# Decoder trunk step on one core: query columns first, cache pages on a fixed chunk schedule, value pages in pairs, softmax matmuls beside them, entry in pieces

## The reference, cut to what matters

```python
def branch_inputs(h, w_in, b_f, pos):
    z = h @ w_in
    rq, rk, rv, rg, fq, fk, fv, ff, gr, gf = jnp.split(z, cuts, axis=-1)
    ...
    logf = jax.nn.log_sigmoid(ff.astype(jnp.float32) + b_f.astype(jnp.float32))

def fox_sample(q, k_new, v_new, logf_new, k_past, v_past, logf_past):
    c = jnp.cumsum(jnp.concatenate([logf_past, logf_new], axis=1), axis=1)
    ...
    sc = jnp.concatenate([s_past, s_new], axis=-1) * (D_F ** -0.5) + c_q[..., None] - c_t[:, :, None, :]
    p = jax.nn.softmax(sc, axis=-1)
    return p[..., :p_len] @ v_past + p[..., p_len:] @ v_new

def trunk_layer(h, p, pos, attend, w_in, b_f, gn_g, w_ret_proj, w_fox_proj, w_out, ...):
    o_r, s_new, o_f = attend(rq, rk, rv, fq, fk, fv, logf)
    y_r = (group_norm(o_r) * silu(rg)) @ w_ret_proj
    y_f = o_f @ w_fox_proj
    mix = (sigmoid(gr) * y_r + sigmoid(gf) * y_f) @ w_out
    x1 = layer_norm(ALPHA * h + mix)
    ffn = (silu(x1 @ w1) * (x1 @ w3)) @ w2
    y = layer_norm(ALPHA * x1 + ffn + sigmoid(x1 @ w_pg) * (p @ w_pe))
```

## Time and profile before

| | us |
|---|---|
| median of 3 runs | 1923.43 |
| lowest and highest | 1921.81, 1926.93 |
| profiled execution, device time | 1920.19 |
| its span, first to last instruction | 1918.6 |
| PE busy | 1799.1 (94%) |
| DVE busy | 1024.2 (53%) |
| ACT busy | 777.3 (41%) |
| mean granted clock of PE | 0.978 |
| data moved by DMA | 386.18 MB |

### The profile page before, as it was taken

The page is one execution under the profiler, slowest core; times in us unless marked ns, Lnnn a source line. Parts: engine busy times, 40 slices in busy tenths (PEclk is TensorE's granted clock), DMA queues, the critical chain, the costliest instruction groups (busy, mean ns, idle before and its releaser), DMA issues.

```text
span 1918.6 us, 39299 instructions
## 1 busy us (share of the span) xinstructions
PE 1799.1 (94%) x14307; PEld 1730.0 (90%) x14307; DVE 1024.2 (53%) x2115; ACT 777.3 (41%) x906; POOL 149.1 (8%) x262
## 2 busy tenths in 40 slices
PE   5999989899788989999979999999999999999996
PEld 4999989789777877899969999999999999999995
DVE  5444575665656556456555544444444444444454
ACT  2443433334334333334335455555433334343333
POOL 3340101111122112000000000000000000000000
PEclk9999999899899999999989999999999999999998
DMA  5555667787799999545525555555555655555551
GB/s 159 148 159 162 210 225 249 232 305 239 238 366 334 310 350 338 187 149 186 180 65 176 169 186 176 183 180 180 176 179 177 188 180 175 179 182 166 180 180 46
DMA packets 318256, 386.18 MB, mean 201 GB/s; under 512 B 16376, under 2 KB 293368, under 8 KB 317784
## 3 DMA queue, kind: packets, MB, share of 16 engines
q1 hardware_dynamic: 286832, 287.48, 47.3%
q0 software_dynamic: 28352, 95.84, 14.1%
q10 hardware_dynamic: 2992, 1.79, 0.4%
HBM read 371.21 MB, written 13.84 MB: 201 GB/s over the span
## 4 chain that ended last, share of the span: by engine, by line
PE 79%; DVE 6%; issue 5%; DMA 5%; ACT 3%; POOLq 1%; ACTq 0%; DVEq 0%; POOL 0%; SPq 0%
PE acc L510 24%; PE acc L511 24%; PE acc L515 24%; DMA stateS<-in_state_ret 2%; ACT whi L451 2%; DMA page<-in_cache_v 1%; DVE pagesum L1235 1%; PE X L633 1%; PE X L808 1%; PE X L490 1%; DMA out_ret_state_sample<-stateS 1%; ACT stateS L1004 1%; DVE wlo L456 1%; PE X L483 1%; DVE stateS L1351 0%
## 5 line engine op out<-in xcount | busy, mean ns | idle before, releaser
L456 DVE TENSOR_TENSOR wlo<-raw,whi 128x1024 fp32r<-128x1024 f32 (+1 forms) x552 | 659.5, 1203 | 711.8 <-ACT whi L451 705.6
L451 ACT ACTIVATE whi<-raw 128x1024 fp32r<-128x1024 f32 (+1 forms) x552 | 569.3, 1038 | 701.8 <-PE acc L515 698.8
L510 PE MATMUL acc<-x_hi,whi 128*128 128x264 f32 x1664 | 415.5, 285 | 10.5 <-DVE x_lo L1483 6.8
L511 PE MATMUL acc<-x_lo,whi 128*128 128x264 f32 x1664 | 414.8, 285 | 0.0
L510 PE MATMUL acc<-hT_hi,whi 128*128 128x264 f32 x1408 | 374.9, 300 | 0.0
L511 PE MATMUL acc<-hT_lo,whi 128*128 128x264 f32 x1408 | 362.8, 292 | 0.0
L510 PEld LDWEIGHTS acc<-x_hi,whi 128*128 128x128 f32 x1664 | 313.7, 188 | 11.6 <-issue 7.2
L511 PEld LDWEIGHTS acc<-x_lo,whi 128*128 128x128 f32 x1664 | 315.0, 189 | 0.0
L510 PEld LDWEIGHTS acc<-hT_hi,whi 128*128 128x128 f32 x1408 | 276.1, 196 | 23.3 <-issue 20.2
L511 PEld LDWEIGHTS acc<-hT_lo,whi 128*128 128x128 f32 x1408 | 276.9, 197 | 0.6 <-issue 0.5
L515 PE MATMUL acc<-x_hi,wlo 128*128 128x264 f32 x1664 | 238.9, 286 | 0.0
(11 more groups left out here) (306 smaller groups left out, 1592.7 us busy)
## 6 DMA issues: line engine op xcount, KB each, us to landing
raw<-in_w SPq DMA_DIRECT2D x256, 512.0 KB, 4.0
raw<-in_w_in SPq DMA_DIRECT2D x176, 512.0 KB, 4.9
page<-in_cache_k POOLq DMA_DIRECT2D x64, 512.0 KB, 5.7
page<-in_cache_v POOLq DMA_DIRECT2D x64, 512.0 KB, 6.1
raw<-in_w_out SPq DMA_DIRECT2D x32, 512.0 KB, 4.5
raw<-in_w_pg SPq DMA_DIRECT2D x32, 512.0 KB, 3.5
stateS<-in_state_ret POOLq DMA_DIRECT2D x8, 1024.0 KB, 8.8
out_ret_state_sample<-stateS POOLq DMA_DIRECT2D x8, 1024.0 KB, 6.6
```

Of the source, the lines that this page charges most:

```text
L451: nc.scalar.activation(whi[:, s, 0:k, :], raw[:, s, 0:k, :], ACT.Copy).then_inc(S["hi_made"], 1)
L456: nc.vector.tensor_tensor(wlo[:, s, 0:k, :], raw[:, s, 0:k, :], whi[:, s, 0:k, :].bitcast(F32), ALU.subtract).then_inc(S["lo_made"], 1)
L510: mm(acc[c.acc][:, m, 0:T], w, xh[:, c.kt0 + t, :], start=c.first and t == 0, stop=False)
L511: mm(acc[c.acc][:, m, 0:T], w, xl[:, c.kt0 + t, :], start=False, stop=False)
```

## The change

- A phase `phQ` of 16 chunks does all query columns first; `phKV` (16 to 47) does keys and values. Later phases keep their chunk numbers.
- The laps are replaced by a table of due chunks. For token m the key pages are at chunks 24 + 16m + 1, 3, 5, 7, 9, 11, 12, 13, the bias and maximum at +14, its transpose at +15, the diagonal made at +16 and spread at +19, the exponential at +21, the sums at +22 and +23, the probabilities at +24, and pairs of value pages at +27, +31, +35, +39. The last pair is at chunk 175.
- Key pages have two buffers and value pages two of their own.
- States are handled every 7 chunks from chunk 112, with load at +0, scaling at +3, update and store at +5, use at +6; the sample tail follows at chunks 168 to 175 and `own_values` after the second chunk of `phYR`. The loops of `phG` are unrolled.
- x is loaded in half tiles, sample rows first. ACT computes the sample rows' mean and variance. PE does chunks 0 to 3 between the transposes, then the forget logits as 48 matmuls with the 8 columns of `wff` as weights.
- The 64 `Lc` loads are issued by SP, eight after each weight load from 4 to 11, instead of by POOL.

```diff
+FIRST, LAP = 24, 16
+KEY_AT = (1, 3, 5, 7, 9, 11, 12, 13)
+BIAS_AT, TURN_AT, TOP_AT, ROWS_AT, LESS_AT, EXP_AT, SUM_AT, SUMS_AT, PROB_AT = 14, 15, 16, 19, 20, 21, 22, 23, 24
+VALUE_AT = (27, 31, 35, 39)
+STATE0, STATE_LAP = 112, 7
+SCALE_AT, NEW_AT, OUT_AT = 3, 5, 6
...
-        phF = Phase(plan, 2, heads([FK, FQ, FV], 512, ready=lambda k: ("h_lo", k)))
+        phQ = Phase(plan, 1, heads([FQ], 1024, ready=lambda k: ("h_lo", k)))
+        phKV = Phase(plan, 2, heads([FK, FV], 512))
...
+            for j in range(len(phQ.chunks)):
+                load(phQ, 0, j)
+                if j == 4:
+                    sp.wait_ge(S["ptab_in"], 16)
+                if 4 <= j < 12:
+                    for i in range((j - 4) * 8, (j - 3) * 8):
+                        number = sp.value_load(ptab[0:1, i:i + 1], min_val=0, max_val=NPOOL - 1)
+                        sp.dma_start(Lc[:, i, :], a["cache_logf"][ds(number, 1)].rearrange("o s h -> s (o h)")).then_inc(S["past_in"], 16)
...
+            def forget_logits():
+                pe.wait_ge(S["h_made"], DT)
+                pe.wait_ge(S["wff_made"], 1)
                 for k in range(DT):
-                    last = mm(X[0:n, 0, t * 8:t * 8 + 8], h32[:, k, lo:lo + n], wff[:, k, :], start=k == 0, stop=k == DT - 1)
-            last.then_inc(S["ff_ps"], 1)
...
+                    mm(X[0:H_F, 0, 0:T], wff_hi[:, k, :], hT_hi[:, k, :], start=k == 0, stop=False)
+                    mm(X[0:H_F, 0, 0:T], wff_hi[:, k, :], hT_lo[:, k, :], start=False, stop=False)
+                    last = mm(X[0:H_F, 0, 0:T], wff_lo[:, k, :], hT_hi[:, k, :], start=False, stop=k == DT - 1)
+                last.then_inc(S["ff_ps"], 1)
...
+            def sample_step(c):
+                for n, at in enumerate(VALUE_AT):
+                    m = due(c, at)
+                    if m is not None:
+                        past_values(m, 2 * n)
+                        past_values(m, 2 * n + 1)
+                m = due(c, TURN_AT)
+                if m is not None:
+                    past_max_T(m)
...
+            h_tiles(0, 8)
+            for j in range(len(phQ.chunks)):
+                multiply(phQ, 0, j)
+                if j == 0:
+                    h_tiles(8, 12)
+                if j == 1:
+                    h_tiles(12, 16)
+                if j == 3:
+                    forget_logits()
+                    side_rows()
+                if j == 4:
+                    forget_rows()
...
-            act.wait_ge(x_in[1], 16)
+            act.wait_ge(x_in[0], 16)
...
+            xs, rest = xtok[0:DEC, 2, :], h32[0:DEC, 0:8, :].rearrange("p k t -> p (k t)")[:, 0:D]
+            link.step(A(rest, xs, ACT.Copy, accum_out=stat[0:DEC, 50:51]))
+            link.step(A(stat[0:DEC, 51:52], stat[0:DEC, 50:51], ACT.Copy, scale=-1.0 / D))
+            link.step(A(rest, xs, ACT.Square, bias=stat[0:DEC, 51:52], accum_out=stat[0:DEC, 52:53]))
...
+            h_rows(0, 4)
+            split_lo(dve, phQ, 0, 0)
+            h_rows(4, 8)
+            normalise(2)
+            split_lo(dve, phQ, 0, 1)
+            normalise(3)
...
+            def load_key(n):
+                if n >= 2:
+                    pool.wait_ge(S["page_used"], HEADS + (n - 1) * H_F)
+                number = pool.value_load(ptab[0:1, n:n + 1], min_val=0, max_val=NPOOL - 1)
+                pool.dma_start(page[:, n % 2, :], a["cache_k"][ds(number, 1)].rearrange("o s c -> s (o c)")).then_inc(page_in[n % 2], 16)
+
+            def load_value(n):
+                if n >= 2:
+                    pool.wait_ge(S["pv_ps"], n)
+                number = pool.value_load(ptab[0:1, n:n + 1], min_val=0, max_val=NPOOL - 1)
...
+                k = state_due(c, 0)
+                if k is not None:
+                    load_state(k)
+                k = state_due(c, NEW_AT)
+                if k is not None:
+                    store_state(k)
```

More of the change, by code:

```diff
@@ L53, with due, state_due @@
           "sc_made": 1, "r_res": 1, "g_lo_made": 1, "pv_ps": 1, "st_ps": 1}
[L57 to L73, removed]
+FIRST, LAP = 24, 16
[4 more added lines that the diff above has]
+SCALE_AT, NEW_AT, OUT_AT = 3, 5, 6
+LAST_STATE = STATE0 + 7 * STATE_LAP + OUT_AT
+def due(c, at, first=FIRST, lap=LAP):
+    m, rest = divmod(c - first - at, lap)
+    return m if rest == 0 and 0 <= m < 8 else None
+def state_due(c, at):
+    return due(c, at, STATE0, STATE_LAP)
 def shape_constants(SEQ, DEC, PAST, H_R):
@@ L517, in multiply, with fox_query_rows @@
                 last.then_inc(S["multiplied"], 1)
+            def fox_query_rows():
+                pe.wait_ge(S["p_made"], 1)
+                pe.wait_ge(S["f_evac"], 4)
+                for i in range(H_F):
+                    last = tr(X[0:DEC, 2 + i // 4, i % 4 * P:(i % 4 + 1) * P], qT8[:, i, SEQ:T], ident)
+                last.then_inc(S["f_ktok_ps"], 1)
             def fox_key_rows(it):
@@ new lines, in _ @@
+            for j in range(len(phQ.chunks)):
+                split_hi(act, phQ, 0, j + AHEAD)
+                if j == 3:
+                    side_hi()
+                if j == 5:
+                    forget_logs()
+                if phQ.chunks[j].last:
+                    group_done(act, phQ, 0, j)
+                    i0, ac = j // 4 * 2, phQ.chunks[j].acc
+                    A(qT8[:, i0:i0 + 2, :], acc2(ac), ACT.Copy, scale=QS).then_inc(free[ac], 1)
+                    act.wait_ge(free[ac], phQ.group(0, j) + 2)
+                    A(qS[:, i0:i0 + 2, :], qT8[:, i0:i0 + 2, SEQ:T], ACT.Copy).then_inc(S["f_evac"], 1)
@@ new lines, in _ @@
+            for j in range(len(phQ.chunks)):
+                split_lo(dve, phQ, 0, j + AHEAD)
+                if j == 3:
+                    side_lo()
+                if j == 5:
+                    forget_rows()
+                if j == 6:
+                    forget_made()
+                if j == 8:
+                    V.memset(probZ[:, :, :, :, :].rearrange("s p g b t -> s (p g b t)"), 0.0)
+                    link.step(V.memset(qZ[:, :, :, :].rearrange("s h d b -> s (h d b)"), 0.0))
@@ L1176, in _ @@
+            for it in range(phKV.iters):
+                for j in range(len(phKV.chunks)):
+                    split_lo(dve, phKV, it, j + AHEAD)
                     if it == 1 and j == 2:
                         fox_result(0)
-                    if it == 1 and j == 6:
+                    if it == 1 and j == 4:
                         dve.wait_ge(S["decay_ps"], 1)
@@ L1677, in _ @@
+            pool.wait_ge(S["f_store_k"], 64)
             pool.wait_ge(S["f_store_v"], 64)
```

887 lines of the change are left out of this document (462 added, 425 removed).

## The result

The changed kernel takes 1912.4 us (median of 6 runs, 1910.8 to 1918.4) against 1924.0 for the kernel before on the same chip: ratio 0.9947, 95% interval 0.9932 to 0.9962. It is 0.5% faster, where 2.4% was predicted. The profiled execution spans 1911.3 us against 1918.6, 7.3 less; the prediction had 1873.6.

What follows compares the result with a forecast made beforehand. TensorE, busy 94%, was taken to bound the kernel, with gains only where it idles or runs at its lower clock. Span 1918.6 - 93 + 24 + 20 + 4 = 1873.6, predicted time 1877 us, range 1840 to 1915.

Steps and rivals of the forecast that it cites:

- DMA in the gate stage, +20: Chunks 112 to 175: full transfers (+14) and a state loop of 25.3 us against 24.2 cost 20, bounds 5 and 40.
- Softmax waits, 52: Eight laps: moving maximum, diagonal and sum matmuls apart removes PE's waits on VectorE, gaining 52 us.
- Value pages, 26 and 4: Laps' ends: earlier requests and paired pages remove PE's DMA waits, gaining 26 us; 32 fewer insertions gain about 4.
- Tail, own values, new scores, 11: Around chunks 175 and 176, own values and new-token scores: moving these steps gains 4.3, 3.5 and 3.3 us, together 11.
- The 93 as a whole: Whole kernel: gains of 52, 26, 4 and 11 us make 93 with nothing new waiting, a span of 1825.6.
- Entry by itself, -5: Start of kernel: chunks 0 to 3 between transposes and shorter forget logits bring chunk 4 to about 60 from 65.0.
- Log-forget pages on SyncE, +24: Entry: 64 small loads at 1.15 us each delay SP's weight loads, chunk 16 starting at 124.5 instead of 100.2.
- Rivals A, B and D: In turn: SP's loads cheap, 1848 us, chance 0.20; SP's loads dear, 1957, 0.10; neither SP nor DMA binding, 1828, 0.05.
- Key page 7, +4: Each lap: page 7, requested two chunks before use, makes VectorE wait about 2.5 us; cost 4, bounds 0 to 15.
- The last line of the sum: Whole kernel: span 1873.6 becomes execution 1875.2, the runs' median lies 3.2 above that, predicted 1877 us.
- rival C: Fixed schedule makes its own waits, state loop and POOL's blocking at the upper bounds, +35: 1912 us, chance 0.13.
- the forecast's 222: Gate stage, chunks 112 to 175: PE's time without DMA waits, the forecast 242 us less 20.

Runs made afterwards that it cites:

- experiments 4 to 6: The changed kernel with a second retention-state buffer (1896.3 us), with most key and value pages loaded at a quarter of their columns (1890.4), and with both (1866.7).
- experiment 6: The changed kernel with a second state buffer and key and value pages, from the third of each sort, cut to a quarter of their columns: 1866.7 us.
- experiment 11: The changed kernel with the softmax steps of laps 1 to 7 close together again, the probabilities still written in chunk 24 of the lap: 1946.5 us.
- experiment 9: The changed kernel with value pages used one at a time instead of in pairs every fourth chunk: 1937.3 us.
- experiment 1: The changed kernel with the 64 log-forget loads taken from SyncE's weight queue and given to POOL: 1880.6 us.
- experiments 4, 7 and 8: The changed kernel with a second state buffer (1896.3 us), with ScalarE's state scaling one chunk later (1906.6), and with POOL's state steps ahead of page loads (1899.9).
- two_states: The changed kernel with a second retention-state buffer and the loads of states 2 to 6 five chunks earlier, state 1 beside state 0: 1896.3 us.
- small_pages: The changed kernel with key and value pages, from the third of each sort, loaded with 256 of 1024 columns: 1890.4 us.
- experiment 12: The changed kernel with log-forget loads on POOL and a second state buffer, state 1 loaded two chunks behind state 0: 1866.7 us.
- the last three: The changed kernel with log-forget loads on POOL and two state buffers (1866.7 us), that with state steps ahead of pages (1867.7), that with state loads in quarters (1865.6).

## Why the prediction was wrong

The direction, the place of the loss and most terms were right. The size was not: 0.5% instead of 2.4%. The step that failed is the DMA term of the gate stage, +20.

- **DMA in the gate stage, +20.** The prediction priced the bytes at +14 and found a state loop of 25.3 us against 24.2 for seven chunks, 1.1 too long a turn. It took 20 as a value between two readings and did not say how the two combine. The loop takes 30.9 a turn: 9.2 from the store to the next load (8.5 to its landing) instead of 6.6, and 7.1 instead of 4 for splits, semaphores and POOL's page loads in front of the store. So it is 6.7 too long a turn, 47 us over the seven turns, and not 8. And the two limits nearly add, as the table of experiments 4 to 6 shows: 19.3 for the bytes and 22.1 for the one buffer, 35.6 together. The stage took 271.9, where 242 was forecast. 7 of these 30 are waits for value pages, so by difference the term measured some 43 instead of 20, just beyond its upper bound of 40. (The 35.6 hold those 7 too; 14 us of the stage stay even in experiment 6.)
- **Softmax waits, 52.** No wait is left at the three lines, and experiment 11 gives a net 2.4 a stall, 58 for 24.
- **Value pages, 26 and 4.** Half right. Waits of 15.5 remain instead of none. 8.4 of them stand in the retention stage (the worst two behind chunk 83, with a chunk at 1.2 GHz after them), and that is its miss: with small pages it takes 244.9, where 245 to 250 was forecast. Pairs against singles are 25 by experiment 9, but no run prices the insertions alone, the 4.
- **Tail, own values, new scores, 11.** Right. The tail cost 5.5 behind chunk 175 and slowed the chunk after it; now its steps cost about 2 in chunks 168 to 171 (4.3 was forecast as the gain). The two chunks around the old place of the own values lost 3.7, and 0.2 is left at the new one (3.5 forecast). The new scores cost 2.1 over a plain chunk instead of 5.4 (3.3 forecast). That chunks 176 to 191 took 5 less than the 52 needs no other term: eight value pages stood there before, with 0.7 each, and none does now.
- **The 93 as a whole.** From chunk 16 to the end experiment 6 takes 1737.9 us, the kernel before 1818.4. That is 80.5 less with 14.0 of waits for states and pages left, 94.5 together. So the part of the sum that rested on PE's own waits came out.
- **Entry by itself, -5.** Right within what can be told: with POOL doing the loads chunk 16 starts at 95.0, where 100.2 - 5 was forecast. Its parts were off: transposes start at 27.5, not 24.2, chunk 0 at 34.1, not 31.
- **Log-forget pages on SyncE, +24.** Right, 28.3 at chunk 16, and 32 of the time by experiment 1. A load costs 1.14, where 1.15 was taken: POOL's unrolled page loads were the right row for the price. Rivals A, B and D fell. The 4 us too few are the later start (weight load 4 at 32.7 instead of 29.3).
- **Key page 7, +4.** VectorE waits 8.3 us for key pages in all, and PE never waits for a maximum. No cost shows.
- **Chunks 16 to 47** were taken as unchanged. The new scores moved here from chunk 53 and cost 2.1 in chunk 43, and the transposes of the second group's probabilities (L588) wait 1.5 in chunk 46: +4.
- **The last line of the sum** slipped: 1875.2 and 3.2 are 1878, not 1877. It changes nothing.

The measured time is that of **rival C** to the microsecond, 1912, "the state loop and POOL's blocking at the upper bounds". Its mechanism is what experiments 4, 7 and 8 show: one buffer, a ScalarE that stands in order, a POOL that issues the store behind pages. It is not the whole of it, as two_states and small_pages say: the other part is the sum of bytes. It had a chance of 0.13, when ScalarE already waited up to 5.80 for a state in the trace of before, in a loop with one chunk more to spare; now it waits up to 11.4. That C meets the number is also partly luck, since entry, pages and the key pages missed by several us in both directions.

What stays open: eight chunks a state instead of a second buffer was not tried, since the state tail would no longer end inside the stage. And of the 14 us between the forecast's 222 and the 236.3 of experiment 6, 10.2 is PE's wait at the first state, where two states, a row and pages are asked for within a few us. Two chunks between the first two states did not remove it (9.3 in experiment 12); an earlier place for state 0 was not tried. That the bytes and not some other effect of the large pages make the weights late rests on experiment 5 and on the sum at 378 GB/s; no run changed the weights' own traffic.

The fastest versions here are the last three, which tie at 1865.6 to 1867.7. The simplest of them, lf_two, is 3.0% faster than before and 2.4% faster than the change as it was made.

## What to carry over

When a transfer and an in-order engine form a loop through one buffer, write its turn down as a sum of all its legs and compare it with the time the schedule gives it. A store that took 6.6 us in the old trace took 8.5 in the new, so take such legs near their upper end. Where a loop and a bandwidth limit are equally close, do not take the larger one and call the other covered: here they came near to adding (19.3 and 22.1 gave 35.6). Removing one alone gave less than half of what both gave (16.3 and 13.5 of 35.6). A queue that issues all weights has a budget, namely how far it runs ahead of the engine that eats them. Small loads are free up to it and cost in full beyond.

## What the runs showed of the hardware

- A load of 4 KB whose address comes from a register load costs SyncE 1.14 us on average and 1.10 in the fastest groups; without the register load it costs 0.49.
- The profile's releaser can be two steps from the cause. "PE waits for VectorE's state" was 31.7 us after and 24.3 with the second buffer; behind the turn shown of the first stood a late state, behind the longest of the second two late weights. Follow the waiting engine's own queue before naming a cause.
- The core's DMA engines moved more than 380 GB/s in several stretches of 10 us of the kernel after, and up to 393 (675 to 685). One of them:

```profile
527.00:537.00 10.00, 4.92 (x41) 4.71 (x39) 6.14 (x26) 3.63 (x6) 2.02 (x4) 0.94 1.06 382
```

and PE was busy less than half of these 10 us.
